# Causal mask of the score maxima added by VectorE in a hybrid encoder step, with values of two cycles issued together

## What is computed

```python
def fox_block(q, k, v, cq, ck, q_pos, k_pos):
    s = jnp.einsum('bqhd,bkhd->bhqk', q, k).astype(jnp.float32) * (HEAD_DIM ** -0.5)
    s = s + jnp.swapaxes(cq, 1, 2)[..., :, None] - jnp.swapaxes(ck, 1, 2)[..., None, :]
    mask = k_pos[None, :] <= q_pos[:, None]
    p = jax.nn.softmax(jnp.where(mask, s, -jnp.inf), axis=-1)
    return jnp.einsum('bhqk,bkhd->bqhd', p.astype(v.dtype), v)
...
def mixer_layer(x, w, fox_attend, h0_re, h0_im, mem_k, mem_v):
...
    fox_out = fox_attend(fq, fk, fv, logf).reshape(B, T, FOX_WIDTH) * jax.nn.silu(fg)
    ssm_out = ssm_y * jax.nn.silu(sg)
    mem_out = memory_attention(mq, mem_k, mem_v).reshape(B, T, MEM_WIDTH) * jax.nn.silu(mg)
    mix = jnp.concatenate([fox_out, ssm_out, mem_out], axis=-1) @ w_out
    return x + mix, fk, fv, logf, h_re, h_im
```

## Time and profile before

| | us |
|---|---|
| median of 3 runs | 1453.31 |
| lowest, highest | 1453.03, 1454.95 |
| the profiled execution's own time | 1454.54 |
| its span | 1452.8 |
| PE busy | 1397.1 (96%) |
| DVE busy | 976.3 (67%) |
| ACT busy | 610.5 (42%) |
| POOL busy | 553.5 (38%) |

### The profile page before, as it was taken

The page is one execution under the profiler, slowest core; times in us unless marked ns, Lnnn a source line. Parts: engine busy times, 40 slices in busy tenths (PEclk is TensorE's granted clock), DMA queues, the critical chain, the costliest instruction groups (busy, mean ns, idle before and its releaser), DMA issues.

```text
span 1452.8 us, 24958 instructions
## 1 busy us (share of the span) xinstructions
PE 1397.1 (96%) x8510; PEld 1105.9 (76%) x8510; DVE 976.3 (67%) x1827; ACT 610.5 (42%) x1220; POOL 553.5 (38%) x580
## 2 busy tenths in 40 slices
PE   8999999999999989999998899999999999899998
PEld 8999767788877767777776677777777777578886
DVE  4789754782566787655334577787786767987774
ACT  6766422432434363435332344444444445431221
POOL 1121433100043252112003366776776658534442
PEclk9999999999999999999999899999999999899999
DMA  7884799986279587788983935726627432446552
GB/s 226 305 285 174 249 235 254 317 258 193 84 181 350 162 263 254 256 276 275 329 274 103 259 74 113 149 49 128 133 51 153 93 62 66 140 161 200 185 186 89
DMA packets 207565, 275.82 MB, mean 190 GB/s; under 512 B 49424, under 2 KB 146096, under 8 KB 203952
## 3 DMA queue, kind: packets, MB, share of 16 engines
q1 hardware_dynamic: 206400, 274.22, 64.9%
q10 hardware_dynamic: 1040, 0.00, 0.0%
HBM read 186.93 MB, written 86.00 MB: 188 GB/s over the span
## 4 chain that ended last, share of the span: by engine, by line
PE 55%; DVE 7%; issue 3%; DMA 2%; SPq 2%; ACT 2%; POOL 1%; DVEq 0%; ACTq 0%; POOLq 0%
PE in_g L925 13%; PE attn_pv L2512 8%; PE attn_s L2580 6%; PE attn_s L2481 5%; PE attn_pv L2580 5%; PE attn_s L2486 4%; PE attn_s L2468 4%; DVE attn_acc_v L2782 2%; DVE attn_tops L2818 2%; PE in_b L1100 1%; DMA in_xu<-scratch_xt 1%; DVE attn_den L2844 1%; POOL in_hv L1808 1%; PE attn_s L2475 1%; PE attn_s L2494 1%
## 5 line engine op out<-in xcount | busy, mean ns | idle before, releaser
L925 PE MATMUL in_g<-in_wh,in_xh 128*128 128x512 f32 (+2 forms) x904 | 331.4, 380 | 5.4 <-DVE in_wl L1519 1.9
L925 PE MATMUL in_g<-in_wl,in_xh 128*128 128x512 f32 (+2 forms) x904 | 321.9, 369 | 0.0
L925 PE MATMUL in_g<-in_wh,in_xl 128*128 128x512 f32 (+2 forms) x904 | 235.0, 379 | 1.4 <-DVE in_xl L1530 1.3
L2782 POOL TENSOR_TENSOR attn_probs<-attn_probs,attn_probs_turned 128x512 f32<-128x512 f32 (+3 forms) x184 | 196.4, 1067 | 86.9 <-ACT attn_probs_turned L2610 65.6
L2610 ACT ACTIVATE attn_probs_turned<-attn_s 128x512 f32<-128x512 f32 (+1 forms) x352 | 161.5, 544 | 155.9 <-PE attn_s L2486 155.9
L2818 DVE TENSOR_REDUCE attn_tops<-attn_s 128x1 f32<-128x512 f32 (+3 forms) x288 | 159.7, 617 | 94.0 <-PE attn_s L2468 71.5
L925 PEld LDWEIGHTS in_g<-in_wh,in_xh 128*128 128x128 f32 x904 | 165.5, 189 | 39.7 <-issue 6.3
L925 PEld LDWEIGHTS in_g<-in_wl,in_xh 128*128 128x128 f32 x904 | 165.6, 189 | 28.0
L925 PEld LDWEIGHTS in_g<-in_wh,in_xl 128*128 128x128 f32 x904 | 158.0, 189 | 34.8 <-issue 5.2
L1806 POOL TENSOR_SCALAR in_hs<-in_hs 128x8 f32<-128x8 f32 (+1 forms) x53 | 19.7, 372 | 401.8 <-DVE in_hs L1557 401.8
L2512 PE MATMUL attn_pv<-attn_probs_turned,attn_v 128*64 128x256 f32 (+1 forms) x1216 | 146.3, 371 | 0.0
(11 more groups left out here) (380 smaller groups left out, 2756.2 us busy)
## 6 DMA issues: line engine op xcount, KB each, us to landing
in_xu<-scratch_xt SPq DMA_DIRECT2D x87, 512.0 KB, 5.3
in_xl<-scratch_xt SPq DMA_DIRECT2D x34, 512.0 KB, 4.5
in_raw<-in_w_in SPq DMA_DIRECT2D x40, 256.0 KB, 5.4
scratch_xt<-in_xu SPq DMA_DIRECT2D x19, 512.0 KB, 4.5
scratch_xt<-in_xl SPq DMA_DIRECT2D x17, 512.0 KB, 5.0
scratch_k<-in_x_turned SPq DMA_DIRECT2D x17, 512.0 KB, 7.2
scratch_q<-in_x_turned SPq DMA_DIRECT2D x17, 512.0 KB, 5.4
in_x_turned<-in_x_prompt SPq DMA_DIRECT2D x16, 512.0 KB, 4.9
```

What stands on the lines that cost most here:

```text
L925: last = X.matmul(g_ps[b][:, 0:m], x, ws[:, c, w0:w0 + m], start=(c == 0 and h == 0 and ws is wh), stop=(c == KC - 1 and h == 1))
L2782: E.tensor_tensor(acc[:, part:, :], acc[:, part:, :], mine, ALU.add).then_inc(added[engine], 1)
```

## The change

- The mask product of the maxima (L2471) is gone. DVE takes the maximum over the blocks ahead of the diagonal one as before, and a new instruction for the diagonal block: it adds `causr` to it, writes the sum back to PSUM, and puts its maximum into a fifth column of `top_parts`. A unit's −max is then made by two small reductions, for tile 0 and for tiles 1 to 3, also in the fox0 units, which had none.
- `TOGETHER = 2`: dens and values of two cycles are issued after the second, values unit by unit, `copied` right behind its unit.
- `late` holds for fox12 alone: in head 7 four of fox8's twelve blocks are added on DVE and eight on POOL.
- The three hooks stand after parts 1 and 2 of the last visit and after the projection's order instead of after its parts 0, 1 and 2, and SP's first loads (now `sync_begin`) are issued at the first hook.
- t_split and t_low of the first two sums come a cycle earlier and ahead of gated(0); product(0,1) comes ahead of the last unit's den.

```diff
--- before.py
+++ after.py
...
-    for n in range(HOOKS):
-        beside[NV - 1, n] = [("attention", n)]
-    order = projection_order(items, visits, behind, beside)
+    for n in range(HOOKS - 1):
+        beside[NV - 1, n + 1] = [("attention", n)]
+    order = projection_order(items, visits, behind, beside) + [("attention", HOOKS - 1)]
...
                     sp.dma_start(dst, src).then_inc(K.s_early, 16)
+                if what == "attention" and n[0] == 0:
+                    K.begin[0](sp)
                 if what == "x":
...
 UNITS = (("fox", 0), ("fox", 4), ("mem", 0), ("mem", 4), ("fox", 8), ("fox", 12))
-CYCLE = 4
+CYCLE, TOGETHER = 4, 2
...
         for u in units:
-            late = u.head == FOX_HEADS - 1 and u.first >= 8
+            late = u.head == FOX_HEADS - 1 and u.blocks > 12
             mine = [k for k, _ in u.scores if u.kind == "fox" and (late or u.blocks > 8 and k in (2, 3, 6, 10))]
...
     first = next(c for c in range(cycles) if scores[CYCLE * c][0].head == FOX_HEADS - 1)
-    ended = {}
+    ended, waiting = {}, []
     for c in range(cycles):
         mine = range(CYCLE * c, CYCLE * (c + 1))
-        if c - 1 in ended:
-            order += [("copied", u) for u in ended[c - 1]]
         order += [("scores", b) for b in mine]
...
         order += [("add", b) for b in mine]
-        if c - 2 in ended:
-            order += [("den", u) for u in ended[c - 2]]
-        order += [("values", b) for b in mine]
         ended[c] = [n for n in range(len(units)) if CYCLE * c < score_end[n + 1] <= CYCLE * (c + 1)]
         order += [("both", n) for n in ended[c]]
+        waiting += mine
+        if c % TOGETHER == TOGETHER - 1 or c == cycles - 1:
+            order += [("den", n) for e in range(c) if e + 2 <= c for n in ended[e] if ("den", n) not in order]
+            for n in sorted({scores[b][0].n for b in waiting}):
+                order += [("values", b) for b in waiting if scores[b][0].n == n]
+                if score_end[n + 1] <= waiting[-1] + 1:
+                    order.append(("copied", n))
+            waiting = []
         if 1 <= scores[CYCLE * c][0].head <= KC // 2 and scores[CYCLE * c][:2] == (units[len(UNITS) * scores[CYCLE * c][0].head + 4], 8):
...
             order += [("w_split", n - 1, 0), ("w_split", n - 1, 1), ("w_low", n - 1)]
+        if n in (KC, KC + 1):
+            order += [("t_split", n - KC), ("t_low_early", n - KC)]
         if n == KC + 1:
             order.append(("gated", 0))
-        if n in (KC + 1, KC + 2):
-            order += [("t_split", n - KC - 1), ("t_low_early", n - KC - 1)]
     assert rows == len(units) and upto == len(tops) and not ended[cycles - 2]
-    order += [("copied", n) for n in ended[cycles - 1]]
-    order += [("product", 0, 0)] + [("den", n) for n in ended[cycles - 1]]
-    order += [("product", 0, 1), ("first_sum", 0), ("t_split", 2), ("t_split", 3), ("mix", 1)]
+    order += [("product", 0, 0), ("product", 0, 1)] + [("den", n) for n in ended[cycles - 1]]
+    order += [("first_sum", 0), ("t_split", 2), ("t_split", 3), ("mix", 1)]
...
-    joined = [sum(1 for u in units[:n + 1] if u.kind == "fox" and u.first) for n in range(ALL)]
+    joined = [sum(1 for u in units[:n + 1] if u.kind == "fox") for n in range(ALL)]
...
         probs = a.sb("probs", [P, 2, 4, 4, P])
-        top_parts, negmax = a.sb("tops", [P, 2, EACH, 4]), a.sb("negmax", [P, 2, EACH])
+        top_parts, negmax = a.sb("tops", [P, 2, EACH, 5]), a.sb("negmax", [P, 2, EACH])
         den = a.sb("den", [P, 2, EACH])
...
-        def sync_program(sp):
+        def sync_begin(sp):
             sp.wait_ge(K.s_cleared, 1)
...
+        def sync_program(sp):
             sp.wait_ge(*K.end_products)
...
                         else:
-                            masked = k + n == u.first + i + 1
                             last = X.matmul(bank[:, at:at + n, :], qb[h][0:LANE, q], kb[h][0:LANE, keys],
-                                            start=True, stop=not masked)
-                            if masked:
-                                last = X.matmul(bank[:, at + n - 1, :], identr[:, :], causr[:, :], start=False, stop=True)
+                                            start=True, stop=True)
                     last.then_inc(s_mx, 1)
...
                     bank = ring_ps[ring.at[what, s]]
-                    alone, last = u.kind == "mem" or u.first == 0, s + 1 == top_end[u.n + 1]
+                    last, d = s + 1 == top_end[u.n + 1], joined[u.n] % 2
                     dve.wait_ge(s_mx, s + 1)
-                    if (alone or last) and u.n >= 2:
+                    if (u.kind == "mem" or last) and u.n >= 2:
...
                         dve.wait_ge(s_diag, u.n - 1)
-                    if alone:
-                        many = len(parts)
-                        V.tensor_reduce(negmax[:, u.n % 2, i:i + many], bank[:, 0:many * n, :].rearrange("p (x n) k -> p x (n k)", x=many),
+                    if u.kind == "mem":
+                        V.tensor_reduce(negmax[:, u.n % 2, i:i + 2], bank[:, 0:2 * n, :].rearrange("p (x n) k -> p x (n k)", x=2),
                                         AX.X, ALU.max, negate=True).then_inc(s_top, 1)
...
-                            dve.wait_ge(s_neg, joined[u.n] - 2)
-                        V.tensor_reduce(top_parts[:, joined[u.n] % 2, i, k // 4:k // 4 + 1],
-                                        bank[:, 0:n, :].rearrange("p n k -> p (n k)"), AX.X, ALU.max).then_inc(s_top, 1)
+                            dve.wait_ge(s_neg, 2 * (joined[u.n] - 2))
+                        with_diag = k + n == u.first + i + 1
+                        whole = n - with_diag
+                        if whole:
+                            done = V.tensor_reduce(top_parts[:, d, i, 1 + k // 4:2 + k // 4],
+                                                   bank[:, 0:whole, :].rearrange("p n k -> p (n k)"), AX.X, ALU.max)
+                        if with_diag:
+                            done = V.tensor_tensor_reduce(out=bank[:, n - 1, :], in0=bank[:, n - 1, :], in1=fl(causr[:, :]), scale=1.0,
+                                                          scalar=-3e38, op0=ALU.add, op1=ALU.max, accum_out=top_parts[:, d, i, 0:1])
+                        done.then_inc(s_top, 1)
                     if last:
                         dve.wait_ge(s_top, s + 1)
-                        if not alone:
-                            V.tensor_reduce(negmax[:, u.n % 2, :], top_parts[:, joined[u.n] % 2, :, 0:u.first // 4 + 1],
-                                            AX.X, ALU.max, negate=True).then_inc(s_neg, 1)
-                            dve.wait_ge(s_neg, joined[u.n])
+                        if u.kind == "fox":
+                            for x, m in ((slice(0, 1), u.first // 4 + 1), (slice(1, EACH), u.first // 4 + 2)):
+                                V.tensor_reduce(negmax[:, u.n % 2, x], top_parts[:, d, x, 0:m],
+                                                AX.X, ALU.max, negate=True).then_inc(s_neg, 1)
+                            dve.wait_ge(s_neg, 2 * joined[u.n])
                         if u.n >= 2:
...
-        K.begin = None, tensor_begin, None, vector_begin
+        K.begin = sync_begin, tensor_begin, None, vector_begin
         return sync_program, tensor_program, scalar_program, vector_program, gpsimd_program
```

## The result

The changed kernel takes 1457.86 us (median of 18 runs, 1456.31 to 1463.12), the kernel before, run beside it, 1453.75. The ratio is 1.0029 with a 95% interval of 1.002 to 1.0039: slower by 4 us where 19 less had been forecast, and outside the range. The profiled execution has a span of 1457.4 us where the one before had 1452.8.

The account below looks back on a forecast made before the run. PE's instructions were taken to bound attention, 56.3 of 56.7 us a head. Start -9.5, heads 0 to 6 -5, last head -8.4, +2 and +2 sum to -18.9: 1434 us from a median of 1453.31, range 1415 to 1446.

Parts of the forecast that it names:

- What bounds it, and the prices of single steps: Attention heads: PE's instructions set the time; mask product 0.11 us, values block entered and left 0.35, masked maximum on VectorE 0.35.
- What comes back: Heads 0 to 6: PE waits for VectorE at rows and memory pairs return 21 us of 26 saved, bounds 0 to 26.
- -5: Heads 0 to 6: net gain of 5 us, from 26 us less PE work and 21 given back.
- at 1.9 in all: Row of fox12: PE stands 1.2 us, more if VectorE comes late or a den's bank is unread; 1.9 taken.
- My 0.98 for the diagonal: Fox12's row: VectorE's time for the diagonal, 0.98 us, within the 4.4 it needs after the last four tops.
- The last head, -8.4: Last head: waits of 2.14 and 1.68 us, 1.65 of clock, 1.0 of entries and 1.9 of values saved.
- VectorE is ahead: Last head: seven of fox8's sums go to GpSimd, so PE's den waits of 2.14 and 1.68 us vanish.
- The start, -9.5: Start of attention: earlier loads let PE resume at 795.3 instead of 804.9, with the same half-clock loss, gaining 9.5 us.
- The tail, +4: End: GpSimd's seven additions ahead of the gating cost 2 us, half clock after PE's longer load wait 2.
- the slower one, 1460: Rival: VectorE becomes the bound, masked maxima costing 1.0 us at fox8's diagonal; 1460 us, chance 0.06.
- GpSimd is late in the last head: Rival: in the last head all 7.9 us of GpSimd's additions precede gating and first mix; 1440 us, chance 0.08.
- Operation and read: Rival: masked maximum and accumulator read lie end to end on VectorE, 2.2 us more a head; 1441 us, chance 0.10.

Follow-up runs that it names:

- b_hmd_split_8_4: Kernel before plus later hooks, earlier loads, masks on VectorE, den ahead of adds, four of fox8's twelve head-7 blocks on GpSimd: 1433.38 us, ratio 0.9846.
- b_masks: Kernel before with only the maxima's masks moved to VectorE: 1457.39 us, ratio 1.0024.
- b_masks_den: Kernel before with the masks on VectorE and, in every cycle, the den ahead of the adds: 1446.03 us, ratio 0.9945.
- b_late: Kernel before with only four instead of twelve of fox8's head-7 blocks added on VectorE, eight on GpSimd: 1459.67 us, ratio 1.0037.
- the best version: Kernel before with later hooks, earlier loads, masks on VectorE, den ahead of adds, fox8's head-7 blocks split eight VectorE, four GpSimd: 1433.38 us.

## Why the prediction was wrong

- **What bounds it, and the prices of single steps: right.** A block of values costs 0.36 less as half of a group (forecast 0.35). The masked maximum takes VectorE 0.21, under the 0.35 that I took and under the row of its size. In b_hmd_split_8_4 a head is 1.3 us shorter than before for 1.76 of masks; part of the rest is waits of 0.3 and 0.5 us that came in.
- **"What comes back", 21 us of 26 in heads 0 to 6: wrong, and the step that failed first.** Between the 23rd exponential and head 7 the changed kernel loses 7.2 us where I had -5. Two things were missing. The clock: I priced every wait of PE at its own length, though rows 10 and 12 both showed half clock behind waits. Four stretches of 1.7 us are 6.8 of the 12.2. The other 5.4 follow by subtraction and aren't split further: between the two marks PE is not busy for 16.7 us, 2.1 before, and a delay shorter than the overlap of two products doesn't show as idle time (four products that last 1.10 at 1232.92 last 1.25 at 984.61). I walked through the waits with VectorE on time at the start of a cycle and named the bank of a den as "more", at 1.9 in all. b_masks and b_masks_den show what that bank costs in the ungrouped order, where it is the main wait, and that its length is set by what stands between it and VectorE's last maximum: diagonal and addition, 1.76 each beside GpSimd. In the changed kernel the diagonal and the banks of maxima are waited for as well, 5.9 and 4.8 us against 3.2 for the banks of dens. My 0.98 for the diagonal was one row of many: in the kernel before they last 0.69 to 1.60. The place of the bank's wait could be seen there too, at 0.22:

```profile
1027.06 0.98 PE L2464 MATMUL attn_s<-attn_mkb,attn_mqb 66*128 66x256 f32 x6 [0.22 <-DVE attn_den L2844]
```

- **The last head, -8.4: wrong by 10.** I took "VectorE is ahead" from its having seven additions less, put PE's two waits at nothing, and costed GpSimd's seven as a delay of the gating. The sum of fox8 is joined from both engines, so VectorE's queue stands until the slower one is done, and with it every den behind the join. The waits are 6.26 us instead of none (3.82 before); b_late alone shows 3.99 where 1.68 stood. Behind the longest the clock fell for 3.4 us.
- **The start, -9.5: right in its mechanism, 2.6 too much.** The store went at 783.33 (forecast 783.4), the first load at 783.85 (783.9), PE reached the memory maxima at 795.32 (795.3). What was mis-sized is the clock. I assumed the same loss behind it; it is 8.0 us against 3.5, because PE now works through the whole stretch. A wait of 1.38 at 816.77 for maxima and the stretch at 818.6 behind it came on top, and masks and blocks of values saved ahead of the 23rd exponential gave some of it back.
- **The tail, +4: +2.5.**
- **The rivals.** The time came out near the slower one, 1460, but not by its mechanism: that needs 0.9 us or more for a masked maximum, and it is 0.21. "GpSimd is late in the last head" came true in part: VectorE's join waits 2.93 for it and PE 4.45 at 1265.08 for its gating, though the tail as a whole lost only 2.5. Operation and read did not lie end to end. The Trainium skill, "VectorE: DVE Perf Modes", section "The DRAIN you can't avoid", has the next operation wait until the pipe is empty, but also says that one that isn't held starts earlier, which I had left out. Here an operation of 0.288 is followed after 0.21, and that fits the second sentence. The Trainium skill, "SBUF — State Buffer", section "Who interferes with whom", has an operation with one input from SBUF free of GpSimd and one with both from there hindered by a GpSimd instruction that reads SBUF: here the trace agrees on both sides, 0.288 on average over all 128 masked maxima, and diagonals and additions of up to 1.76 in b_masks at 906.24 and 907.92, of 0.69 and 0.68 with GpSimd idle. This was the rule that mattered, and I used it for the added operation alone instead of for those that stand between PE and its bank.
- **The missing rival** was this one: PE waits for the reader of a bank, once or twice a head and for 1 to 2 us, and the clock makes it dearer. It needs no engine to be the bound; VectorE still had 10 to 14 us of room in each of heads 1 to 6 of the changed kernel.

What stays open: what makes a wait be followed by a drop or not. At 986.88 and 1009.16 there is none behind waits of 1.0. Why grouping costs 16.7 us alone and 36 on the best version, but only 3 to 4 beside the masks and `late`, is argued from where the waits stand and not shown. No run took the hooks back out of the changed kernel.

## What to carry to other kernels

An engine at 96% with another at 70% isn't safe from the other: look at what the second does between the instruction that the first waits for and the one ahead of it, and put the reader of a shared buffer in front of work that nobody waits for. Two steps exchanged in that order were worth 11 us in the ungrouped kernel, three times what the masks cost without it. Work that looks like overhead, such as many short blocks instead of few long ones, may be the cover for another engine's latency; before grouping it, walk through the longest chain of the other engine with its slow durations, not its means. And count a wait of TensorE with the half clock that may follow it.

## What the runs showed of the hardware

- A drop of the granted clock to 0.50 came behind PE waits of 1 to 2 us, in stretches of 3.4 and 6.8 us, though PE was busy for 52.3 of the 56 us from 1084 to 1140 in the changed kernel; in b_masks four times in heads 1 to 4, each at a wait of 1.85 to 1.95 us, in b_masks_den, with 0.29 there and 0.55 at most elsewhere, never.
- The read of VectorE's accumulator costs nothing of its own: in all 128 cases of the changed kernel it starts 0.21 us behind its operation, and where VectorE needn't wait the next operation starts together with it (1008.97).
- An addition of 512 columns with both inputs in SBUF takes VectorE 0.68 us with GpSimd idle and often longer beside it: 1.76 in b_masks at 907.92, 2.92 before, and once 5.37 (b_late at 1229.13). A maximum of 128 columns from PSUM plus mask stays at 0.28 to 0.30 either way.
